# Six buffers instead of four for the gathered key rows of an expert layer

## The reference, cut to what matters

```python
def retrieve(xt):                                    # 128 tokens at a time
    q = xt @ w_q                                     # 8 heads x 2 halves x 128
    s = einsum("thpc,hpkc->thpk", q, sub_keys)
    s1, i1 = top_k(s[:, :, 0], 16); s2, i2 = top_k(s[:, :, 1], 16)
    ...                                              # the best 16 of the 256 sums of pairs
    gate = softmax(top_s)                            # and idx = i1 * 128 + i2 of each
    u, v = expert_u[idx], expert_v[idx]              # 16384 experts, rows of 1024
    act = gelu(einsum("thkd,td->thk", u, xt))
    return einsum("thk,thkd->td", gate * act, v)
```

## Time and profile before

| | |
|---|---|
| median of 3 runs | 4057.33 us (4053.84 to 4060.56) |
| the profiled execution | 4050.34 us |
| its span, first to last instruction | 4048.6 us |
| TensorE (PE) busy | 3860.2 us, 95% |
| VectorE (DVE) busy | 2609.8 us, 64% |
| ScalarE (ACT) busy | 1593.7 us, 39% |
| GpSimd (POOL) busy | 548.3 us, 14% |
| moved by DMA | 702.09 MB, mean 173 GB/s |
| the forty steps | about 3014 to 3437 us |
| the value stage | about 3510 to 4030 us |

### The profile page before, as it was taken

One profiled execution on the slowest core, in us unless ns is written; L12 is line 12 of the kernel. 1 busy time (PEld: TensorE's weight loads), 2 busy tenths in 40 slices (PEclk: granted clock), 3 DMA queues, 4 the chain that ended last, 5 costly groups with the idle time before them and its releaser, 6 DMA issues. The chain is left out here.

```text
span 4048.6 us, 54428 instructions
## 1 busy us (share of the span) xinstructions
PE 3860.2 (95%) x19449; PEld 3235.0 (80%) x19449; DVE 2609.8 (64%) x4778; ACT 1593.7 (39%) x2228; POOL 548.3 (14%) x565
## 2 busy tenths in 40 slices
PE   7999999998999989998999999999999999999998
PEld 6888786876888878876668887668889999988886
DVE  6642776765662556337854324768997788678787
ACT  3222335334322332225853222533345555533333
POOL 1100000000110011000100000000014455233332
PEclk9999999999999999998999999989999999999999
DMA  7632421322652256322012222113358999899997
GB/s 285 227 135 83 152 87 47 109 94 79 237 199 104 98 193 218 125 90 76 1 63 96 102 94 83 63 42 117 126 177 320 346 328 332 324 353 352 355 349 278
DMA packets 140677, 702.09 MB, mean 173 GB/s; under 512 B 18631, under 2 KB 20006, under 8 KB 95022
## 3 DMA queue, kind: packets, MB, share of 16 engines
q1 hardware_dynamic: 66574, 424.29, 29.4%
q0 software_dynamic: 73952, 275.81, 18.6%
HBM read 637.06 MB, written 59.80 MB: 172 GB/s over the span
## 5 line engine op out<-in xcount | busy, mean ns | idle before, releaser
L112 DVE TENSOR_TENSOR w_lo<-raw,w_hi 128x2048 fp32r<-128x2048 f32 x331 | 758.7, 2292 | 695.8 <-ACT w_hi L104 684.0
L124 PE MATMUL ps<-x_hi,w_hi 128*128 128x512 f32 (+1 forms) x2768 | 1032.2, 373 | 35.6 <-DVE w_lo L112 31.1
L125 PE MATMUL ps<-x_lo,w_hi 128*128 128x512 f32 (+1 forms) x2768 | 1022.3, 369 | 0.0
L126 PE MATMUL ps<-x_hi,w_lo 128*128 128x512 f32 (+1 forms) x2768 | 1022.1, 369 | 0.0
L104 ACT ACTIVATE w_hi<-raw 128x2048 fp32r<-128x2048 f32 x331 | 633.4, 1914 | 647.2 <-PE ps L126 412.8
L124 PEld LDWEIGHTS ps<-x_hi,w_hi 128*128 128x128 f32 x2768 | 520.9, 188 | 111.7 <-issue 35.1
L125 PEld LDWEIGHTS ps<-x_lo,w_hi 128*128 128x128 f32 x2768 | 521.0, 188 | 68.0
L126 PEld LDWEIGHTS ps<-x_hi,w_lo 128*128 128x128 f32 x2768 | 520.6, 188 | 68.3
L2419 POOL DMA_INDIRECT ph_rows<-in_peer_u,ph_names x128 | 226.6, 1770 | 1248.7 <-DVE ph_names L2789 988.4
L2502 PE MATMUL ps<-w_hi,px_gh 128*128 128x512 f32 x768 | 299.0, 389 | 1.9 <-issue 1.5
L2502 PE MATMUL ps<-w_lo,px_gh 128*128 128x512 f32 x768 | 298.8, 389 | 0.0
(11 more groups left out here) (423 smaller groups left out, 5559.5 us busy)
## 6 DMA issues: line engine op xcount, KB each, us to landing
raw<-in_slabs SPq DMA_DIRECT2D x331, 1024.0 KB
ada_ring<-in_w_ada POOLq DMA_DIRECT2D x160, 512.0 KB, 5.4
act_dram<-px_act SPq DMA_DIRECT2D x64, 384.0 KB
gate_dram<-ps_g SPq DMA_DIRECT2D x12, 2048.0 KB
px_g<-gate_dram POOLq DMA_DIRECT2D x32, 768.0 KB, 7.6
px_ai<-act_dram POOLq DMA_DIRECT2D x64, 384.0 KB, 6.5
h_dram<-h SPq DMA_DIRECT2D x2, 2048.0 KB
h<-h_dram SPq DMA_DIRECT2D x2, 2048.0 KB, 8.5
```

Of the source, the lines that this page charges most:

```text
L112: nc.vector.tensor_tensor(k.wlo[:, c % 2, :], k.raw[:, c % 2, :], k.whi[:, c % 2, :].bitcast(F32), ALU.subtract).then_inc(k.raw_free, 1)
L124: mm(out, hi, rhs_hi, start=start, stop=False)
L125: mm(out, hi, rhs_lo, start=False, stop=False)
L126: return mm(out, lo, rhs_hi, start=False, stop=stop)
```

## The change

The ring of four is kept for the tail and the value rows. For the first 120 key rows (`N_WIDE` = 40 x 3, as many as the forty steps have dots) the gathers go through six buffers (`WIDE` = 6): the four of `rows`, and rows 0 and 1 of `h_tok`. Six further semaphores tell of the landings. Gather n of these waits for dot n - 6. Gathers 120 to 123 go back to the ring of four and also wait for dot n - 6. From 124 on it is dot n - 4 again. The start issues six gathers, the tail's first batch two fewer. ScalarE waits for 120 dots before it first writes `h_tok`.

```diff
+WIDE = 6
+N_WIDE = 40 * OPS_SPREAD
+        wide_in = list(signals(k, ctx, "px_", [f"wide{j}" for j in range(WIDE)]).values())
+
+        def row_of(n):
+            if n >= N_WIDE:
+                return rows[:, (n - N_WIDE) % ROWS, :]
+            return rows[:, n % WIDE, :] if n % WIDE < ROWS else h_tok[:, n % WIDE - ROWS, :]
+
+        def row_signal(n):
+            return row_in[(n - N_WIDE) % ROWS] if n >= N_WIDE else wide_in[n % WIDE]
...
-                    if n >= ROWS:
+                    if n >= N_WIDE + ROWS:
                         gp.wait_ge(s["row_used"], n - ROWS + 1)
+                    elif n >= WIDE:
+                        gp.wait_ge(s["row_used"], n - WIDE + 1)
...
-            gather(ROWS)
+            gather(WIDE)
             for n in range(40):
                 gather(OPS_SPREAD)
-            gather(OPS_TAIL[0])
+            gather(OPS_TAIL[0] - (WIDE - ROWS))
...
                 for r in range(NBD):
                     act.wait_ge(s["ht"], NBD * half + r + 1)
+                    if half == 0 and r == 0:
+                        act.wait_ge(s["row_used"], N_WIDE)
...
-                ve.wait_ge(row_in[n % ROWS], 16 * (turns * i + n // ROWS + 1))
+                past = (n - N_WIDE) // ROWS if n >= N_WIDE else n // WIDE
+                ve.wait_ge(row_signal(n), 16 * (turns * i + past + 1))
...
-                row = rows[:, n % ROWS, :]
+                row = row_of(n)
```

More of the change, by code:

```diff
@@ L2416, in gather @@
                 for n in range(asked[0], min(asked[0] + count, N_OPS)):
-                    if n >= ROWS:
+                    if n >= N_WIDE + ROWS:
                         gp.wait_ge(s["row_used"], n - ROWS + 1)
-                    gp.indirect_dma_start(rows[:, n % ROWS, :], None, d["peer_u" if n < P else "peer_v"],
-                                          bass.IndirectOffsetOnAxis(names[:, n % P:n % P + 1], 0)).then_inc(row_in[n % ROWS], 16)
+                    elif n >= WIDE:
+                        gp.wait_ge(s["row_used"], n - WIDE + 1)
+                    gp.indirect_dma_start(row_of(n), None, d["peer_u" if n < P else "peer_v"],
+                                          bass.IndirectOffsetOnAxis(names[:, n % P:n % P + 1], 0)).then_inc(row_signal(n), 16)
                     asked[0] = n + 1
             gp.wait_ge(s["names"], HEADS)
-            gather(ROWS)
+            gather(WIDE)
             for n in range(40):
                 gather(OPS_SPREAD)
-            gather(OPS_TAIL[0])
+            gather(OPS_TAIL[0] - (WIDE - ROWS))
             gp.wait_ge(s["g_free"], 12 + 2)
@@ L2819, in row_ready @@
             def row_ready(turns, i, n):
-                ve.wait_ge(row_in[n % ROWS], 16 * (turns * i + n // ROWS + 1))
+                past = (n - N_WIDE) // ROWS if n >= N_WIDE else n // WIDE
+                ve.wait_ge(row_signal(n), 16 * (turns * i + past + 1))
             def dot(turns, i, n):
                 row_ready(turns, i, n)
-                row = rows[:, n % ROWS, :]
+                row = row_of(n)
                 V.scalar_tensor_tensor(row, row, 1.0, x_tok[:], ALU.mult, ALU.mult,
-                                       accum_out=dots[:, bass.ds(turns * ROWS * i + n, 1)]).then_inc(s["row_used"], 1)
+                                       accum_out=dots[:, bass.ds(turns * WIDE * i + n, 1)]).then_inc(s["row_used"], 1)
             def add_row(turns, i, n):
@@ L2831, in add_row @@
                 ve.wait_ge(s["row_used"], turns * ROWS * i + n)
-                V.scalar_tensor_tensor(acc, rows[:, n % ROWS, :], wts[:, bass.ds(turns * ROWS * i + n - P, 1)], acc,
+                V.scalar_tensor_tensor(acc, row_of(n), wts[:, bass.ds(turns * ROWS * i + n - P, 1)], acc,
                                        ALU.mult, ALU.add).then_inc(s["row_used"], 1)
@@ L2880, in step @@
                 for m in range(OPS_SPREAD):
-                    dot(8 * OPS_SPREAD // ROWS, i, OPS_SPREAD * n + m)
+                    dot(8 * OPS_SPREAD // WIDE, i, OPS_SPREAD * n + m)
             def last_step(n):
```

## The result

| | before | after |
|---|---|---|
| median | 4053.84 us (5 runs, 4051.36 to 4060.56) | 4034.48 us (5 runs, 4032.26 to 4037.17) |
| ratio | | 0.9948, 95% interval 0.9938 to 0.9959 |
| profiled execution, span | 4050.34, 4048.6 us | 4034.48, 4032.6 us |

The change is faster by 21 us (0.0052 x 4054), between 17 and 25 by the interval of the ratio. The two medians lie 19.4 us apart, the means of the same runs 20.7. The prediction was 18.2 us faster and a time of 4039.1, which is 4.6 us above the measured one. The 4039.1 stood on a median of three runs, 4057.33. With two more runs that median is 4053.84.

The account below looks back on a forecast made before the run. TensorE was taken as the bound, with 18.8 us of holes from late key rows; -18.5 for holes and +0.3 for semaphores gave -18.2, so 4039.1 us from 4057.33; own range 4035 to 4044, 8-in-10 range 4034 to 4049.

Parts of the forecast that it names:

- The sum: Whole kernel: -18.5 us for holes plus 0.3 for semaphores, -18.2 us, from the median 4057.33 to 4039.1.
- The bound and the size of the holes: Forty steps: TensorE sets the pace; they take 423.05 us where 404.3 would do, an excess of 18.8 us.
- The remainder of 0.3 us: First of the forty steps: holes expected to stay, so 18.5 us of gain was taken, not 18.8.
- none of it is clock: Forty steps: the granted clock is at its upper level, so no part of the 18.8 us excess is clock.
- Why rows are late: Key gathers: release four rows back allows 9 us for a trip of 12; six buffers remove all 60.4 us of waits.
- The allowance: Third gather of a bunch with six buffers: 20.2 - 4.55 = 15.7 us, 1.6 more than the longest trip, 14.1.
- VectorE's 1.73 us to spare: Each of the forty steps: VectorE without waits takes 8.38 us against TensorE's 10.11, so it can lose 1.73 us.
- The longest trips lie next to a gate store: Key gathers: argument for the rival that transfer engines become the bound, or trips stretch at 2 MB gate blocks; chance 0.13.
- Do the transfers keep up: Forty steps: 3.54 MB in 10.11 us needs 350 GB/s with engines 0.95 busy; it fits, narrowly.
- transfer bound: Rival, forty steps: transfer engines become the bound and half the excess, 9.4 us, stays, giving 4048.2 us; chance 0.13.
- slabs starve: Rival: gather bytes delay slabs, 3 us at each of ten gate stores, 30 us added, giving 4069 us; chance 0.07.
- The small edits: Start, tail and end: six semaphores cost 0.3 us; first gathers, the tail's batch and ScalarE's wait cost 0.

Follow-up runs that it names:

- the table's first four rows: Kernel before (profile), the same once more, with six unused semaphores, and with six buffers released as with four; steps 423.05, 423.6, 426.9, 424.5 us.
- the two kernels with reductions: Changed kernel with one or two unused 1024-element VectorE reductions added in each of the forty steps; ratios to before 0.9946 and 1.0000.
- the kernel at 408 GB/s: Changed kernel with each step's activations stored two more times, 768 KB more a step; ratio to before 0.9984, steps 416.9 us.
- Half rows: Kernel before with four buffers, each key gather bringing 512 of 1024 elements; whole time not comparable, steps 404.27 us.
- six semaphores more: Kernel before with six more semaphores that are only made and cleared; one run, steps 426.9 us.

## Which step of the prediction failed, and what held

**The step that failed is the base in "The sum"**, 4057.33 us, "the median of the runs shown". The mechanism held, and the sizes in that sum were off. Both the forecast of 4039.1 and the low end of its range, 4035, stand on that base, and the measured 4034.48 lies 4.6 us under the one and just under the other (the wider range, down to 4034, just holds it). Three runs were too few for it: five put the median at 4053.84, and 17 others at 4053.81. That is 3.5 of the 4.6 us. The prediction took the three runs' scatter of 3.4 us into its range, but left the base itself where it was. The other 1.1 us go the way of the second mis-sized term, the holes; the medians scatter too much to split them further.

**The bound and the size of the holes** were right for the execution they were read from. "The excess is 18.8 us": after the change it is 0.00, in both profiles. TensorE was idle for only 15.0 us of the 18.8; the other 3.8 go with its 14 holes, 0.27 us each, which the prediction left unexplained. The remainder of 0.3 us that I kept for the first steps did not exist. But "none of it is clock" holds for that execution alone. In the table's first four rows, all with the release four rows back, the holes are 18.8, 19.3, 20.3 and 22.6 us, 20.3 on average, and in two of them the lower clock behind a hole is part of it. So the term was 18.5 and measures 20.3; with -20.3 + 0.4 = -19.9 us the sum stands inside the interval of 17 to 25. A profile shows one execution, and this one was the mildest of the four.

**Why rows are late** was right: it is the release. With six buffers and the release of four, nothing is gained. The allowance was right in kind: 15.7 us against trips of 14 predicted no wait, and none was left. Five back already empties TensorE's holes, which also confirms VectorE's 1.73 us to spare, as do the two kernels with reductions (one fits, two do not). What the prediction did not see is that the shortage is made by the order of the dots. Three in a bunch leave two of the three gathers little more than a step, and let them go close together with a slab; with the bunch the median trip is 9.8 us and without it 7.1. Spread out, four buffers suffice.

**"The longest trips lie next to a gate store"** told half. Without those blocks the dots' waits fell only from 60 to 47 us, but the holes from some 20 to 8, and the median trip from 9.8 to 7.8 us. Half the row bytes took the waits to 6 and the holes to none. A third part of a trip is GpSimd's own. In the earlier trace rows the gather started at 3099.33 takes 3.06 us, and the one at 3055.49 takes 0.94. The first starts with this w_lo of VectorE's timeline before:

```profile
3099.28 2.29 DVE L112 TENSOR_TENSOR w_lo<-raw,w_hi 128x2048 fp32r<-128x2048 f32 x1
```

With the dots spread out, 73 of 119 gathers start while VectorE is idle, 42 with or in a short one_hots instruction and 4 in w_lo. GpSimd's timeline in that kernel:

```profile
3097.63 0.94 POOL L2419 DMA_INDIRECT ph_rows<-in_peer_u,ph_names  x1 [2.94 <-DVE ph_rows L2826]
3100.16 0.94 POOL L2419 DMA_INDIRECT ph_rows<-in_peer_u,ph_names  x1 [1.59 <-DVE ph_rows L2826]
```

Its 120 gathers keep GpSimd busy for 121 us, where the changed kernel's 117 take 220. The Trainium skill, "SBUF — State Buffer", section Who interferes with whom, says that a VectorE instruction with two inputs in SBUF holds up a GpSimd instruction that reads SBUF; the gather reads its row names there, w_lo has two such inputs, and the trace agrees, with 3.06 against 0.94 us. The mean instruction fell from 1.79 us to 1.01, which is 0.8 of the 2.7 us that the median trip fell (an estimate, as it sets a mean beside a median). Half rows removed the waits without this part. No run changed it alone.

**Do the transfers keep up** was right with the wrong measure. I read 0.95 busy as 5% of room and gave "transfer bound" 13%. At a share of 1.00 the stretch still carried 385 GB/s without loss. Where the rate alone would bind is not shown: the kernel at 408 GB/s loses 12.7 us, but part of that is SyncE's order. The Trainium skill's 341 GB/s for a transfer of 1 MB ("DMA: Bandwidth & Descriptors", section Bandwidth), taken as the limit for several transfers in flight, would have given 4049.9; as such a limit it doesn't hold here, with 348 GB/s and no hole. The rival "slabs starve" named the right place: with two more stores w_hi waits for slabs and the dots wait for nothing. But it took more stores in SyncE's list, and this kernel goes 37 GB/s below a rate at which nothing is lost.

**The small edits.** Six semaphores: 0.3 us predicted, 0.43 measured. The wait put before ScalarE's copy costs nothing: the copy runs at 3473.03 and the 120th dot began at 3420.51. The value stage takes 523.2 us in both.

## What to carry to other kernels

Work out the time that a transfer into a reused buffer has: from the release of the buffer to the next use, in steps of the bounding engine, less the time to issue. If consumers stand in a bunch, spreading them over the step may give the same as more buffers, and the transfers themselves got shorter here as well. A wait on an engine that isn't the bound costs only what exceeds its spare time per step, so size the gain by the bounding engine's holes (here 18.8 us), not by the waits (60.4 us); a hole of 1.9 to 3.8 us can cost more than its length when the clock falls behind it. Take the base of a forecast from more runs than three when the gain is as small as their scatter. And when more traffic slows a kernel, look whether the transfers are slow or are issued late.

## What the runs showed of the hardware that was not expected

- The share of busy transfer engines grows more slowly than the rate: 0.94 at 348 GB/s, 1.00 at 385, 1.02 at 408. So 0.95 did not mean 5% of room.
- Within a stretch that is otherwise at the upper level, a hole of 2.96 us was followed by matmuls at the lower one, and the hole and the slow stretch together cost 4.8 us (six semaphores more). Its second slow stretch followed a hole of 1.90 us, while one of 1.91 us in the first profile of the kernel before was not followed by one. So the length of the hole alone doesn't settle it, and what does stays open.
- A gather's instruction takes 0.94 us while VectorE is idle, 1.68 us in the median when it starts within a dot, and 3.06 us when it starts together with w_lo (kernel before). One that starts 0.17 us ahead of w_lo still takes 0.94 (dots spread out, 3103.85).
- A hole costs TensorE some 0.3 us more than the time it is idle. This is an estimate from excess less idle time over the number of waits: (18.8 - 15.0) / 14 = 0.27 in the kernel before, (19.3 - 15.3) / 14 = 0.29 once more, (20.0 - 9.7) / 37 = 0.28 with two reductions more.
